# First layer opened by feature chunks, and layer 1's shift and scale as TensorE column products

## The chip, the cores and the metric

The kernel runs on one core of one Trainium2 chip. The metric is the device time of one execution in microseconds.

## The reference, cut to what matters

The whole program is two layers of `hybrid_layer` (the first block), followed by a second block of feed-forward and mixer stages that the change leaves alone. 256 rows, 1024 features, float32. Each of the two layers computes:

```python
def hybrid_layer(x, c, positions, norm_g, w_ada, b_ada, w_in, ...):
    mod = jax.nn.silu(c) @ w_ada + b_ada                  # (1, 1024) @ (1024, 3072)
    shift, scale, gate = jnp.split(mod[:, None, :], 3, axis=-1)
    h = rms_norm(x, norm_g) * (1 + scale) + shift
    z = h @ w_in                                          # (256, 1024) @ (1024, 2976)
    c_q, c_kv, k_rope, g_mla, q_b, k_b, v_b, g_moba = jnp.split(z, list(IN_OFFSETS), axis=-1)
    o_mla = mla_attention(c_q, c_kv, k_rope, ...)         # 8 heads, latents of 256 and 128
    o_moba = moba_attention(q_b, k_b, v_b, ...)           # 8 heads, one block of 256 keys
    y = concat([silu(g_mla) * o_mla, silu(g_moba) * o_moba]) @ w_out
    return x + gate * y
```

`mod` is one row of 3072 numbers for the whole layer; it needs all of w_ada (12 MB a layer). Its first third is the shift, the second the scale, the last the gate.

## The kernel before, in words

**Precision.** Every large product is made from three products of fp32r operands: x_high w_high + x_high w_low + x_low w_high. ScalarE writes the high part of a weights chunk (`wh`, L906, from `raw`), VectorE the low part (`wl`, L1529). A chunk is 128 partitions by up to 1024 numbers. Activations are split in the same way into `xt_h` (ScalarE) and `xt_l` (VectorE).

**Order of the work.** Each engine has its own program (`pe`, `act`, `dve`, `pool`, `sp`), written out in order; they meet in semaphores. `plan` lists all chunks in the order in which SP's queue loads them into the six `raw` buffers (`sp`, L2564): the load of chunk c waits until chunk c - 6 has been read. A list entry whose last field is set is a piece of w_ada. Such a piece isn't split: VectorE's `weigh` (L1552) multiplies it by a column of silu(c) and adds it to a row accumulator of 128 x 1024 numbers. There are five `wh`/`wl` buffers. `gemm` on TensorE takes the chunks one by one and, for each, the two row halves t = 0, 1 of the activations; results stand in banks 0/1 or 2/3 in turn, and ScalarE evacuates them. Banks 4 to 6 go round for small results (`rot`).

**`side` and `later`** are lists of small steps that all engines' programs hand out at the same points, a rate of steps behind each chunk. `side` carries attention, `later` carries w_ada's work for what comes next.

**The opening of layer 0.** SP loads 16 row pieces of w_ada (8 MB: shift and scale, j = 0 and 2, eight pieces of 1024 columns each), VectorE weighs them into `mkv`, TensorE turns the sums into columns (`turn_row`: four products of a 128 x 128 part with a column of ones each) and makes `keep_busy` products without use in between (5 and 3). x is loaded on ScalarE's queue as one DMA, normalised, transposed (`to_xt`), scaled and shifted per feature chunk into `xtmp`, and split into `xt_h`/`xt_l`. Then come four products one after another over all eight feature chunks: z (416 columns: the latents and k_rope), qb, kb, vb (512 columns each). The rotary tables (`reduce_angle`), head norms (`head_sums`, `head_scale`), the latents' transposes (`to_xt(("c", l) ...)`, `lower_latents`) and the bias table `mbias` are side steps beside these.

**Layer 1's w_ada.** `side_tiles` says what `later` weighs: during layer 0 the pieces (1, 0) into `qt`'s upper half, (0, 4), the gate of layer 0, into `acc`, and (1, 2) into `qkv`'s first rows, eight weighings each; four `turn_row` calls make columns of (1, 0) to (1, 3). During layer 1 the gate (1, 4). Layer 1's first instruction on the normalised rows (`affine`, `turned_row`) needs all its shift and scale.

**The rest of the layer.** Turn of the q and k heads (`turn_heads`), moba attention beside the four short mla products (q0, q1, kv0, kv1: 5 chunks' worth of small products, one take each), the gmla and gmoba gates (four chunks each), mla attention, the gate row and the two `out` products.

Of the kernel before, what the change touches and what calls it, by code (L numbers as in the profile page):

```python
# [15 lines left out]
DM = 1024  # L16
# [234 lines left out]
def build(nc, d, out, ctx):  # L251
# [122 lines left out]
    def stat(n, *name):  # L374

        if name not in stat_of:
# [10 lines left out]
    side_tiles = [[(1, 0), (0, 4), (1, 2)], [(1, 4)]]  # L387
    acc_of = {(0, 0): mkv[:, 0, :], (0, 2): mkv[:, 1, :], (0, 4): acc[:, :], (1, 4): acc[:, :],
              (1, 0): qt[:, 4:8, :].rearrange("p a b -> p (a b)"), (1, 2): qkv[:, 0, 0:DM]}
    acc_free = {(1, 2): ("tr", ("mobak", 0), 2), (1, 4): ("turn", 0, 5)}  # L390
# [9 lines left out]
    def weighed(l, j, kx):  # L400

        return ("acc", l, j + 1 if j < 4 and l == 0 and kx == 7 else j, kx)

    def first_bank_of(c):

        return {0: 2, 2: 3, 4: 7}.get(c)
# [60 lines left out]
    def pe(e):  # L467
# [76 lines left out]
        def to_xt(s, src, nch, ready, by="xl"):  # L544

            for c in range(0, nch, 2):
                m = min(2, nch - c)
                if s == ("x", 0) and first_bank_of(c):
                    b = open_bank(first_bank_of(c), (by, s, c + m - 1))
                else:  # L550
                    b = rot(by, s, c + m - 1)
# [92 lines left out]
        def rows_of_ada(l, j):  # L644

            wv = d["w_ada"][l].rearrange("(c p) n -> p c n", p=128)
            for kx in range(8):
                if len(plan) == c_no[0]:
                    plan.append((wv[:, kx:kx + 1, j * 512:j * 512 + 1024], 1, 1024, None, None, (l, j, kx)))
                c_no[0] += 1  # L650
                yield kx

        def ada(tiles):
            for i, (l, j) in enumerate(tiles):
                for kx in rows_of_ada(l, j):
                    yield
                    if kx < 2 and i:
                        turn_row(tiles[i - 1][0], tiles[i - 1][1] + kx)
                        yield
            for z in range(2):  # L660
                turn_row(tiles[-1][0], tiles[-1][1] + z)
                yield

        def turn_row(l, j):

            if j >= 4:
                return
            b = rot("mod", l, j)
            w.wait_ge(*at("acc", l, j // 2 * 2 if l else j, 7))
            w.wait_ge(*at("ones"))  # L670
            a = acc_of[l, j // 2 * 2][:, j % 2 * 512:j % 2 * 512 + 512]
            for f in range(4):
                last = mm(b[:, f:f + 1], a[:, f * 128:f * 128 + 128], ones[:, 0:1], True, True)
            last.then_inc(*up("turn", l, j))
# [3 lines left out]
        def keep_busy(n):  # L678

            w.wait_ge(*at("x"))  # L680
            for _ in range(n):
                mm(banks[0][:, 0:256], ident, h[:, 0, 0:256], True, True)


        b = rot("ccol")
        w.wait_ge(*at("id"))
        w.wait_ge(*at("c"))
        tr(b[:, 0:8], rows[0:8, :]).then_inc(*up("ctr"))
        list(rows_of_ada(0, 0))
        b = rot("cols")  # L690
        w.wait_ge(*at("rows"))
        tr(b[:, 0:n_rows], rows[0:n_rows, :]).then_inc(*up("rtr"))
        turn_row(0, 0)
        turn_row(0, 1)
        keep_busy(5)
        list(rows_of_ada(0, 2))

        ps, pts = Ring(pb1), Ring(pt1)
        for l in range(NL):
# [12 lines left out]
            else:  # L712
                to_xt(("x", l), lambda c, t: xn[:, t, c * 128:c * 128 + 128], 8, lambda c, t: [("xn", l, t)], by="xh")
                keep_busy(3)
                turn_row(0, 2)
                turn_row(0, 3)
# [4 lines left out]
            def ckey(t, kx):  # L721
                return ("c", l), kx

            later.add(ada(side_tiles[l]), 10 * len(side_tiles[l]))
            later.over(26 if l else 54)
            gemm(("z", l), XT, 0, xkey, win, 0, 416, "eva", head=STAG if l else 1,
                 soon=(lambda: turn_rows(1)) if l else None)
            if l == 0:
                b = rot("relb8")
                w.wait_ge(*at("rel"))  # L730
                w.wait_ge(*at("oh"))
                mm(b[0:8, :], relb[:, :], mq[0:32, 0, 0:512], True, True).then_inc(*up("relmm"))
            gemm(("qb", l), XT, 0, xkey, win, 928, 512, "eva")
            to_xt(("c", l), lambda c, t: z0[:, t, c * 128:c * 128 + 128], 3, lambda c, t: [("zn", l, t, 1)])
            gemm(("kb", l), XT, 0, xkey, win, 1440, 512, "eva")
            gemm(("vb", l), XT, 0, xkey, win, 1952, 512, "eva")
            side.drain()
            if l == 0:
                later.over(17)
# [3 lines left out]
                       lambda t: [("nrm", "kb", l, t)])  # L743
            side.add(attention("moba", l, lambda j: [("qk", ("mobaq", l), j), ("qk", ("mobak", l), j)],
# [19 lines left out]
            for j2 in range(2):  # L764
                o = open_bank(first_bank + j2, ("gate", l, j2))
                w.wait_ge(*at("acc", l, 4, 7))
# [1868 lines left out]
```

## Time and profile before

| | us |
|---|---|
| median of 3 runs | 1601.88 |
| lowest and highest | 1599.12, 2229.82 |
| the profiled execution, its own time | 1596.89 |
| the profiled execution, its span | 1594.7 |
| TensorE, VectorE, ScalarE busy | 1552.5, 1069.9, 869.8 |

The span runs from the first to the last instruction of the core; the execution's own time has 2.2 us more around it. Busy time of TensorE counts the records of its matmuls, which overlap: the distance between the starts of two records, not the length of one, is what a product costs in a stream. A product with float32 operands (not fp32r) leaves two records.

### The profile page before, as it was taken

To read this page: it belongs to the slowest core of one execution; us is meant where nothing else is said; L and a number is where in the kernel's file an instruction comes from. 1 tells how busy PE (TensorE), PEld (TensorE's weight loads), DVE (VectorE), ACT (ScalarE), POOL (GpSimd) and SP (SyncE) were. 2 spreads that over 40 slices of the span, in tenths; PEclk is the share of its full clock that TensorE was granted. 3 is DMA by queue.
4 is the path that set the end of the run, shared out by engine and by line. 5 is a ranking of instruction groups with operands and counts; after the bars stand their busy time and mean duration, and the time that the engine had idled before them with its cause. 6 is when DMAs were issued, how large, how long until landed. Compare 5 with 4: busy or idle time off the path is not lost.

```text
span 1594.7 us, 21371 instructions
## 1 busy us (share of the span) xinstructions
PE 1552.5 (97%) x7540; PEld 1290.8 (81%) x7540; DVE 1069.9 (67%) x1789; ACT 869.8 (55%) x1534; POOL 117.0 (7%) x142
## 2 busy tenths in 40 slices
PE   4989999999999999999999999999999999999998
PEld 4777887788888888888888888888888888888886
DVE  7987877666555766787756557565666578766553
ACT  3676667455445656565644446444566666554442
POOL 0310021011000000021000001000000002100000
PEclk9999999999999999999999999999999999999999
DMA  9964673379854634546565557975463444665651
GB/s 340 322 233 158 196 239 128 104 180 221 222 185 158 198 96 133 174 141 213 197 200 170 198 184 197 199 205 192 158 199 118 139 160 147 211 207 172 205 184 71
DMA packets 149026, 293.03 MB, mean 184 GB/s; under 512 B 10096, under 2 KB 23184, under 8 KB 148920
## 3 DMA queue, kind: packets, MB, share of 16 engines
q1 hardware_dynamic: 143424, 276.60, 51.5%
q0 software_dynamic: 4352, 12.15, 6.2%
q10 hardware_dynamic: 1144, 2.92, 0.5%
q8 instruction: 60, 0.98, 0.2%
q14 instruction: 46, 0.38, 0.1%
HBM read 290.57 MB, written 1.06 MB: 183 GB/s over the span
## 4 chain that ended last, share of the span: by engine, by line
PE 88%; DVE 5%; ACT 3%; issue 2%; DMA 1%; POOL 0%; DVEq 0%; SPq 0%; ACTq 0%
PE pb L475 83%; PE pb L479 5%; DMA raw<-in_w_ada 1%; DVE wl L1529 1%; ACT wh L906 1%; ACT pb L906 1%; DVE mkv L1526 1%; POOL st L2461 0%; DMA raw<-in_w_in 0%; DVE qt L1526 0%; ACT xt_h L906 0%; DVE mk L1529 0%; ACT mkv L906 0%; DVE B L1529 0%; DVE pb L1532 0%
## 5 line engine op out<-in xcount | busy, mean ns | idle before, releaser
L906 ACT ACTIVATE wh<-raw 128x1024 fp32r<-128x1024 f32 (+1 forms) x484 | 506.5, 1053 | 424.6 <-PE pb L475 394.2
L1529 DVE TENSOR_TENSOR wl<-raw,wh 128x1024 fp32r<-128x1024 f32 (+1 forms) x484 | 581.4, 1218 | 197.6 <-ACT wh L906 193.6
L475 PE MATMUL pb<-wh,xt_h 128*128 128x512 f32 (+2 forms) x1472 | 578.1, 393 | 4.0 <-ACT xt_h L906 2.5
L475 PE MATMUL pb<-wh,xt_l 128*128 128x512 f32 (+2 forms) x1472 | 572.4, 389 | 1.4 <-DVE xt_l L1529 1.0
L475 PE MATMUL pb<-wl,xt_h 128*128 128x512 f32 (+2 forms) x1472 | 569.6, 387 | 0.0
L475 PEld LDWEIGHTS pb<-wh,xt_l 128*128 128x128 f32 x1472 | 277.1, 188 | 64.1 <-DVE xt_l L1526 5.9
L475 PEld LDWEIGHTS pb<-wh,xt_h 128*128 128x128 f32 x1472 | 277.2, 188 | 59.5 <-issue 4.0
L475 PEld LDWEIGHTS pb<-wl,xt_h 128*128 128x128 f32 x1472 | 277.4, 188 | 52.5
L475 PE MATMUL pb<-wh,big_h 128*128 128x512 f32 x352 | 137.7, 391 | 0.0
L475 PE MATMUL pb<-wh,big_l 128*128 128x512 f32 x352 | 137.0, 389 | 0.0
L475 PE MATMUL pb<-wl,big_h 128*128 128x512 f32 x352 | 137.0, 389 | 0.0
L2461 POOL TENSOR_TENSOR st<-st,cols 128x1 f32<-128x1 f32 (+2 forms) x56 | 55.6, 1001 | 921.3 <-DVE st L1526 665.7
L475 PEld LDWEIGHTS pb<-wh,big_l 128*128 128x128 f32 x352 | 66.1, 188 | 13.8
L475 PEld LDWEIGHTS pb<-wl,big_h 128*128 128x128 f32 x352 | 66.1, 188 | 13.5
L475 PEld LDWEIGHTS pb<-wh,big_h 128*128 128x128 f32 x352 | 66.1, 188 | 13.4
L1526 DVE SCALAR_TENSOR_TENSOR sgt<-ti,pb 128x512 f32<-128x512 f32 (+1 forms) x48 | 30.3, 642 | 59.0 <-ACT ti L906 59.0
L1526 DVE SCALAR_TENSOR_TENSOR hid<-pb,few,sgt 128x512 f32<-128x512 f32 (+1 forms) x48 | 33.9, 706 | 46.8 <-PE pb L475 46.0
L906 ACT ACTIVATE p<-p,st 128x256 f32<-128x256 f32 x96 | 48.0, 501 | 28.4 <-DVE st L1532 28.4
L906 ACT ACTIVATE pt<-pb 128x512 f32<-128x512 f32 (+1 forms) x80 | 40.2, 502 | 28.8 <-PE pb L479 28.8
L906 ACT ACTIVATE big_h<-pb 128x512 fp32r<-128x512 f32 x44 | 24.1, 596 | 39.0 <-PE pb L479 39.0
L906 ACT ACTIVATE ti<-pb,few 128x512 f32<-128x512 f32 (+1 forms) x48 | 30.8, 658 | 18.4 <-PE pb L475 18.4
L2545 POOL TENSOR_TENSOR G<-G,mg 128x512 f32<-128x512 f32 x14 | 21.8, 1559 | 247.3 <-DVE mg L1526 247.0
(242 smaller groups left out, 1546.5 us busy)
## 6 DMA issues: line engine op xcount, KB each, us to landing
raw<-in_ffn_w_gu SPq DMA_DIRECT2D x160, 512.0 KB, 4.9
raw<-in_w_in SPq DMA_DIRECT2D x148, 512.0 KB, 4.3
raw<-in_ffn_w_down SPq DMA_DIRECT2D x88, 512.0 KB, 3.9
raw<-in_w_ada SPq DMA_DIRECT2D x48, 512.0 KB, 5.3
raw<-in_w_out SPq DMA_DIRECT2D x32, 512.0 KB, 4.1
raw<-in_w_branch SPq DMA_DIRECT2D x24, 512.0 KB, 4.2
raw<-in_ffn_w_gu SPq DMA_DIRECT2D x32, 256.0 KB, 4.9
raw<-in_w_in SPq DMA_DIRECT2D x8, 416.0 KB, 4.8
```

The costliest lines, as they stand in the source:

```text
L475: return e.matmul(o, a, b, start=start, stop=stop)
L479: return e.transpose(o, a, ident[0:n, 0:n])
L906: return e.activation(o, a, func, **kw)
L1526: return e.scalar_tensor_tensor(out=o, in0=a, scalar=s, in1=b, op0=op0, op1=op1)
L1529: return e.tensor_tensor(o, a, b, op)
L2461: e.tensor_tensor(stat(n, "rs", *name), v, halves.to_broadcast([128, n]) if n > 1 else halves, ALU.pow).then_inc(*up("rs", *name))
L2545: e.tensor_tensor(m, m, mg[mg_at(n, n0, t)][:, :], ALU.add).then_inc(*up("mrg", g, t))
```

## The change

The opening goes by feature chunks kx = 0 to 7. For each, SP loads two column blocks of w_ada (128 columns by all 1024 rows, one of the shift and one of the scale, in 512-byte pieces) and the chunk's rows of w_in for z (two chunks together, at even kx) and for q and k (1024 columns). TensorE makes the shift column straight from the raw block (eight products of a 128 x 128 block with a column of silu(c)); VectorE weighs the scale block into two partial sums of 128 x 128 that two products with ones add up. z, q and k are accumulated side by side in banks 0/1, 2/3 and 6/7 and finished together. vb follows, as before by itself. `keep_busy` is gone. x comes first on SP's queue, as two DMAs; ScalarE's rows DMAs are issued before its first Tanh.

Layer 1's shift and scale are 16 column blocks (`next_blocks`) that ScalarE's queue loads into `qkv[:, t, 0:1024]`, the tile of q and k once their heads are turned, two in turn; eight TensorE products make each column (`next_modulation`), as `later` steps from the q0 product on. The gate stays as rows on VectorE.

Around these, `reduce_angle`, gp and the rotary tables move ahead of the head norms, an activation table is loaded behind them, and the latents' transposes move behind the turn of the q and k heads. The core of the diff follows, first the shared tables, then TensorE's program (its `ada`, `next_modulation`, `opening` and the old opening that goes), then ScalarE's (`next_blocks`, `opening`), VectorE's `opening` and SP's first loads:

```diff
+    acc_free = [("modm", 7), ("turn", 0, 5)]
+    next_ada = [qkv[:, t, 0:DM].rearrange("p (c n) -> p c n", n=128) for t in range(2)]
+    N_LATER = (17, 8)
...
+        def ada(l):
+            for i in range(N_LATER[l]):
+                if i < 8:
+                    row_of_ada(l, i)
+                if i and l == 0:
+                    next_modulation(i - 1)
+                yield
+
+        def next_modulation(f):
+            b = rot("modn", f)
+            w.wait_ge(*at(f"next{f % 2}", f))
+            for cc in range(8):
+                last = mm(b[:, 0:1], next_ada[f % 2][:, cc, :], stat(8, "c_silu")[:, cc:cc + 1], cc == 0, cc == 7)
+            last.then_inc(*up("nextm", f))
...
+            for kx in range(8):
+                qk = weights(kx)
+                if kx < 7:
+                    blocks(kx + 1)
+                for t in range(2):
+                    xh, xl = (v[:, kx, t * 128:t * 128 + 128] for v in XT)
...
+                    w.wait_ge(*at("xh", ("x", 0), kx))
+                    for nm, i, c, o, hi, lo in parts:
...
+                        w.wait_ge(*at("hi", c))
+                        mm(o, xh, hi, kx == 0, False)
+                    for nm, i, c, o, hi, lo in parts:
+                        w.wait_ge(*at("lo", c))
+                        mm(o, xh, lo, False, False)
+                    w.wait_ge(*at("xl", ("x", 0), kx))
+                    for nm, i, c, o, hi, lo in parts:
+                        last = mm(o, xl, hi, False, kx == 7)
...
+                    if t == 0 and kx < 7:
+                        modulation_sums(kx + 1, modulation(kx + 1))
...
-        b = rot("cols")
-        turn_row(0, 0)
-        turn_row(0, 1)
-        keep_busy(5)
-        list(rows_of_ada(0, 2))
...
+        def next_blocks(f):
+            w.wait_ge(*at("nextm", f - 2) if f > 1 else at("tr", ("mobak", 0), 2))
+            wa = d["w_ada"][1].rearrange("(c p) n -> p c n", p=128)
+            e.dma_start(next_ada[f % 2], wa[:, :, 128 * f:128 * f + 128]).then_inc(*landed(f"next{f % 2}", f))
...
+            for kx in range(8):
+                w.wait_ge(*at("modk", kx, 1))
...
+                ac_(xt_h[:, kx, :], x_turned[:, kx, :], ACT.Identity, **affine).then_inc(*up("xh", ("x", 0), kx))
+                if kx >= 2:
+                    w.wait_ge(*at("xl", ("x", 0), kx - 2))
+                ac_(xtmp[kx % 2], x_turned[:, kx, :], ACT.Identity, **affine).then_inc(*up("xma", ("x", 0), kx))
+                split(stream.lead(3 if kx % 2 else 4))
...
+            for t in range(2):
+                q_(("qb", 0), t, banks[ACC_Q[t]])
+                squares(("qb", 0, t), qkv[:, t, 0:512], 512, [("eva", ("qb", 0), t)])
+                k_(("kb", 0), t, banks[ACC_K[t]])
+                squares(("kb", 0, t), qkv[:, t, 512:1024], 512, [("eva", ("kb", 0), t)])
+                z_(("z", 0), t, banks[ACC_Z[t]][:, 0:416])
+                split(stream.lead(1))
+            latent_squares(0)
...
+            for kx in range(8):
+                if kx:
+                    modulation(kx)
+                split(stream.lead(1 if kx % 2 else 2))
+                w.wait_ge(*at("xh", ("x", 0), kx))
+                w.wait_ge(*at("xma", ("x", 0), kx))
+                tt(xt_l[:, kx, :], xtmp[kx % 2], xt_h[:, kx, :].bitcast(F), ALU.subtract).then_inc(*up("xl", ("x", 0), kx))
+                if kx < 7:
+                    split(stream.lead(2))
+            split(stream.lead(2))
...
+            reduce_angle(0)
+            reduce_angle(1)
...
+        for t in range(2):
+            e.dma_start(h[:, t, :], d["x"][0, t * 128:t * 128 + 128, :]).then_inc(*landed(f"x{t}"))
```

## Rows read from the trace of the kernel before

**Rows 1.** The page's first part: busy us, share of the span, instructions of each engine

```profile
PE 1552.5 (97%) x7540; PEld 1290.8 (81%) x7540; DVE 1069.9 (67%) x1789; ACT 869.8 (55%) x1534; POOL 117.0 (7%) x142
```

**Rows 2.** Busy time by stretch: length, busy us per engine, TensorE clock, DMA share, GB/s

```profile
0.00:33.80 33.80, 14.28 (x66) 12.69 (x66) 23.08 (x34) 8.44 (x17) 3.98 (x12) 1.00 0.94 357
...
46.80:80.30 33.50, 33.50 (x152) 27.72 (x152) 32.05 (x65) 22.08 (x41) 13.13 (x12) 1.00 0.91 321
83.50:182.50 99.00, 93.08 (x515) 76.39 (x513) 80.94 (x180) 62.74 (x149) 7.92 (x6) 0.98 0.59 197
```

**Rows 3.** TensorE in order of time, 10 to 34 us: start, us, instruction, count

```profile
17.38 0.46 PE L479 MATMUL pb<-cst,rows 120*128 120x120 f32 x1 [11.85 <-DMA rows<-in_mla_k_g]
19.57 3.57 PE L475 MATMUL pb<-ones,mkv 128*128 128x1 f32 x16 [1.73 <-DVE mkv L1526]
...
27.41 2.76 PE L479 MATMUL pb<-cst,ob 128*128 128x128 f32 x16
...
31.31 1.84 PE L475 MATMUL pb<-ones,mkv 128*128 128x1 f32 x16
```

**Rows 4.** TensorE in order of time, 43 to 45 us, in the z product

```profile
43.73 0.46 PE L475 MATMUL pb<-wh,xt_l 128*128 128x416 f32 x1 [0.96 <-DVE xt_l L1529]
44.03 0.35 PE L475 MATMUL pb<-wh,xt_h 128*128 128x416 f32 x1
44.22 0.35 PE L475 MATMUL pb<-wl,xt_h 128*128 128x416 f32 x1
```

**Rows 5.** TensorE in order of time, 47 to 92 us: q product, heads, one turn_row

```profile
47.11 0.39 PE L475 MATMUL pb<-wl,xt_h 128*128 128x512 f32 x1
47.34 0.40 PE L475 MATMUL pb<-wh,xt_l 128*128 128x512 f32 x1
...
80.25 1.04 PE L479 MATMUL pb<-cst,qkv 128*128 128x128 f32 x8
...
90.80 0.95 PE L475 MATMUL pb<-ones,qt 128*128 128x1 f32 x8
91.61 0.48 PE L475 MATMUL pb<-wh,xc_h 128*128 128x512 f32 x1
```

**Rows 6.** Groups by form, 0 to 182.5 us: count, busy us, mean ns, idle before

```profile
L1529 DVE TENSOR_TENSOR wl<-raw,wh 128x1024 fp32r<-128x1024 f32 x29 | 35.1, 1219 | 0.8 <-ACT wh L906 0.8
L906 ACT ACTIVATE wh<-raw 128x1024 fp32r<-128x1024 f32 x29 | 30.4, 1057 | 14.4 <-DMA raw<-in_w_in 9.3 <-PE pb L475 5.2
...
L1526 DVE SCALAR_TENSOR_TENSOR mkv<-raw,st,mkv 128x1024 f32<-128x1024 f32 x12 | 15.4, 1284 | 4.4 <-DMA raw<-in_w_ada 3.6
...
L1526 DVE SCALAR_TENSOR_TENSOR mkv<-raw,st,mkv 128x512 f32<-128x512 f32 x4 | 2.8, 748 | 0.2
```

**Rows 7.** Loads, vectors and powers: queues and engines by time; page's DMA part last

```profile
0.74 22.12 SPq L2579 DMA_DIRECT2D raw<-in_w_ada  x16
...
11.16 0.33 ACTq L1104 DMA_DIRECT2D mq<-in_consts  x1
...
25.05 2.26 ACT L906 ACTIVATE ob<-h,st 128x1024 f32<-128x1024 f32 x2 [9.42 <-POOL st L2461]
...
24.45 1.68 POOL L2461 TENSOR_TENSOR st<-st,cols 128x1 f32<-128x1 f32 x2 [21.30 <-DVE st L1526]
...
raw<-in_w_ada SPq DMA_DIRECT2D x48, 512.0 KB, 5.3
```

**Rows 8.** ScalarE's groups by form, 33 to 182 us

```profile
L906 ACT ACTIVATE kt<-pb,gp 128x512 f32<-128x512 f32 x4 | 2.4, 690 | 1.4 <-issue 1.4
...
L906 ACT ACTIVATE xt_h<-z 128x256 fp32r<-128x256 f32 x4 | 1.4, 406 | 0.0
```

**Rows 9.** VectorE's angle chain from first to next instruction; ScalarE's table load

```profile
59.19 0.17 DVE L1523 TENSOR_SCALAR ang<-ang 128x32 f32<-128x32 f32 x1
...
60.85 1.22 DVE L1529 TENSOR_TENSOR wl<-raw,wh 128x1024 fp32r<-128x1024 f32 x1
...
87.80 1.28 ACT L906 ACT_TABLE_LOAD   x1
```

More of the change, by code:

```diff
@@ L398, in merged_by, with read_out @@
         return ("mrgv" if (n, n0, t) == (2, 512, 0) else "mrg", (s, "y", n, n0), t)
[L400 to L406, printed above, removed]
+    def read_out(what):
+        if what[0] == "shift":
+            return ("shm", what[1])
+        if what[0] == "scale":
+            return ("scs", what[1], 7)
+        return ("acc", *what)
     def moba_unit(l):
@@ L642, in attention, with row_of_ada @@
                 yield
-        def rows_of_ada(l, j):
+        def row_of_ada(l, kx):
             wv = d["w_ada"][l].rearrange("(c p) n -> p c n", p=128)
-            for kx in range(8):
[L648 to L674, printed above, removed]
-        pbuf = {}
[L678 to L682, printed above, removed]
@@ new lines, in pe, with modulation, modulation_sums @@
+        pbuf = {}
+        def modulation(kx):
+            c = shift_at[kx]
+            b = open_bank(4 + kx % 2, ("modk", kx, 1))
+            w.wait_ge(*at(f"raw{c % NRAW}", c))
+            w.wait_ge(*at("csil"))
+            for cc in range(8):
+                last = mm(b[:, 0:1], chunk_view(raw[c % NRAW], c)[:, cc, :], stat(8, "c_silu")[:, cc:cc + 1], cc == 0, cc == 7)
+            last.then_inc(*up("shm", kx))
+            return b
+        def modulation_sums(kx, b):
+            w.wait_ge(*at("ones"))
+            w.wait_ge(*at("scs", kx, 7))
+            for z in range(2):
+                last = mm(b[:, 1:2], part_sums[kx % 2][z], ones[:, 0:1], z == 0, z == 1)
+            last.then_inc(*up("modm", kx))
@@ L1104, in act @@
         e.dma_start(mq[0:32, 0, 0:512], d["consts"][0:32, C_OH:C_ROWS]).then_inc(*landed("oh"))
-        stream.lead(16)
-        rot()
-        turn_row(0, 0)
-        turn_row(0, 1)
+        w.wait_ge(*at("id"))
+        ac_(stat(1, "table"), ident[:, 0:1], ACT.Tanh)
+        w.wait_ge(*at("ccol"))
+        ac_(stat(8, "c_t"), cols[:, 0:8], ACT.Tanh, scale=0.5).then_inc(*up("ctanh"))
         def rows_squares(l, m, ready):
@@ L1216, in act @@
-            for t in range(2):
-                squares(("qb", l, t), qkv[:, t, 0:512], 512, [("eva", ("qb", l), t)])
-            gemm(("kb", l), XT, 8, 512, to(lambda t: qkv[:, t, 512:1024]))
-            for t in range(2):
-                squares(("kb", l, t), qkv[:, t, 512:1024], 512, [("eva", ("kb", l), t)])
-            if l == 0:
+                later.add(ada(l), N_LATER[l])
+                later.over(26)
+                gemm(("z", l), XT, 8, 416, to(lambda t: z0[:, t, :]), head=STAG, between=lambda: turned_row(1))
```

527 lines of the change are left out of this document (272 added, 255 removed).

## The prediction

> **What bounds the kernel now.** I read the page first: TensorE is busy for 97% of the span, VectorE for 67% [rows 1]. Such a share is an average, so the second view is busy time by stretch, cut where the code of the first block changes stage [rows 2]. Up to 33.8 us TensorE has nothing of its own to do: VectorE weighs rows of w_ada (23.1 us busy) and the DMA engines are at 0.94. From 33.8 to 46.8 it has small gaps, from 46.8 to 80.3 none (33.50 of 33.50), and from 83.5 to 182.5 it is idle for 99 - 93.1 = 5.9 us (80.3 to 83.5, the turn of the heads, stands between). So before 33.8 us TensorE time is free; behind it nearly every microsecond given to TensorE lengthens the span, and one taken from VectorE or ScalarE is worth at most part of those 5.9. Third, the order of TensorE's instructions gives the prices [rows 3 to 5]; fourth, ScalarE's and VectorE's groups by form give the chain that feeds it [rows 6, 8].
>
> The sums are made against the profiled execution (span 1594.7, its own time 1596.9, so 2.2 lie around the span). The median of the three runs is 1601.9, 5 us higher.
>
> **The start.** The change takes the h load off ScalarE's queue and puts it as two DMAs at the head of SP's. At one w_ada load every 22.12 / 16 = 1.4 us [rows 7] all raw loads land about 2.8 us later; hidden, because the weighting column c_silu is later still. ScalarE now issues its rows DMAs (5.78 to 11.49, 5.7 us) and the table load (1.28) before its first Tanh, so c_silu comes at about 9.6 instead of 6.4. In exchange the vectors land sooner: the last was issued at 11.2 and its transpose ran at 17.38 [rows 3, 7], 6.2 us on; issued at 7.2 it gives 13.4, with the transpose 14.0. VectorE's order puts cols and the variance behind that: 14.7. Two POOL powers are 1.68, one ScalarE scaling 1.15 (two took 2.26) [rows 7]: 16.7, with the second power beside it. Sixteen transposes at 0.17 (2.76 [rows 3]) end at 19.5. ScalarE's copy goes beside them; two products with ones (0.9 at the speed of the first sixteen) and VectorE's two column instructions (0.45) give shift and scale at 20.9. Then xt_h 0.42 and xtmp 0.33 on ScalarE (0.41 each alone [rows 8], less where they overlap), the z chunk's upper part 0.9, the q/k chunk's 1.0, its lower part on VectorE 1.15, xt_l 0.42, and the last three products of row half 0: 25.8. The modulation of chunk 1 follows. TensorE will then just have left an idle stretch: the sixteen one-column records at 19.57 took 3.57 us, the sixteen at 31.31 took 1.84 [rows 3], which are the levels 1.2 and 2.4 GHz (the view prints a granted clock of 1.00 there, but durations halve). I take something between: 2.4 for the modulation, 0.7 for its sums, modulation 1 ready at 29. The keep_busy products that are removed lay wholly in idle time, 3.5 to 6 us of it, and cost nothing now; without them the first steps run slow, up to 3 us, which is in the 29.
>
> **The eight steps.** One feature chunk is six z products at 0.19 (the spacing of 128x416 [rows 4]) and twelve q/k products at 0.2275 (0.23 in the pair shown [rows 5]): 3.87 us. The modulation adds eight 128x128 by one column products. In full stream eight records (four such products) took 0.81 us, from 90.80 to 91.61 [rows 5], so eight products are 1.65; two sums with ones and the two changes of kind make 0.55. TensorE alone would need 6.07 a step. The program's order is a chain, though. ScalarE makes xt_h, xtmp and only then the upper parts of this chunk's weights; VectorE's lower part follows; TensorE starts the next modulation only behind row half 0, and the next xt_h waits for it. Behind the sums: 0.45 (VectorE columns) + 0.42 + 0.33 + 1.0 + 1.15 + 0.42 + 0.65 (last three products) + 1.65 + 0.45 + some 0.3 of signals = 6.8 on odd chunks; even ones have 832 elements of z weights ahead, + 0.85 = 7.65. VectorE's weighing of a scale block is eight 128x128 instructions; the 512 and 1024 forms (748 and 1284 ns [rows 6]) extrapolate to 0.27 each, 2.15, which fits before the sums. DMA per step is 1.75 MB, 4.9 us at the 357 GB/s of the first 33.8 us [rows 2]. Six steps from 29: 3 x 6.8 + 3 x 7.65 = 43.4, so 72.4; the last chunk's row half 0 ends 4.6 later at 77, half 1 at 79. Before, the same three products (z, q, k) were finished at 69.3: the vb product, 48 x 0.2275 = 10.9, ends at 80.25 [rows 5].
>
> **Behind the steps.** vb uses banks 0 and 1, which hold z, and z is evacuated last on ScalarE, behind q, its squares, k, its squares, for each half. The squares of half 1 need a th tile that VectorE frees by its reduction, and VectorE stands behind two lower parts (2.3), both reduce_angle chains and gp (some 4.6 together: a chain ran from 59.19 to 60.85, 1.66 [rows 9], twice that, and 1.3 for the small instructions around, my estimate; before, they lay beside TensorE's products). That cover is gone: reduction at 84.0, squares, k, squares, z of half 1 at 86.3. vb half 1 starts there, and 9.55 us remain: 95.8 against 80.25, **+15.6**. The latents' transposes now stand behind the q and k heads, whose four kt copies are 2.4 us on ScalarE [rows 8]: first mla product about 5.0 us behind vb instead of 3.3, **+1.7**.
>
> **The layer.** Sixteen modulation columns of layer 1, each 1.65: 26.4 us of TensorE time in the stretch with 5.9 us idle. Removed are four turn_rows of 0.81 to 0.85: 3.4. **+23.0**. Off VectorE go 16 weighings of 0.75 to 1.28, half of them in this stretch; I credit 4 of the 5.9 idle us, with the Exp table load (1.28 at 87.80 [rows 9]) that moves to where vb waits anyway: **-4**. Each column waits for a 512 KB load that ScalarE issues one step earlier, behind the evacuation and the exponentials of that step; raw loads land in 5.3 us (median [rows 7]). In the four short mla products a step is about 4 us of TensorE, so two or three columns wait 2 to 4 us, with VectorE's mod instruction waiting behind and the softmax behind that; in the longer gate products they don't. **+6**, bounds 0 and 12.
>
> Sum: 15.6 + 1.7 + 23.0 - 4 + 6 = 42.3. 1596.9 + 42.3 = 1639 by the profiled execution; a median lies a little higher, so I say **1641**. Unshown operations: loads of 512-byte pieces (nearest: 1664-byte pieces at full rate and 256- to 512-byte vectors in the rows DMAs that took 6 us to land among others), from 0 to + 12 in all, value 0; 1024-piece issues on ScalarE, from 0.33 (the SP issue) to 1 us each, 16 of them beside TensorE work, from 0 to + 5, value 0.
>
> **A rule weighed.** The rows show that a one-column product costs 0.101 us per record in full stream [rows 5]. The Trainium skill (TensorE: Matmul & The Clock Gate, Back-to-back issue gap) gives about 60 cycles, 25 ns, between products of 1 to 64 columns. By it the layer's 256 records would be 6.4 us instead of 26 and the whole 1621, one of the rivals' ends; the trace disagrees, so I give it no more than part of the chance of rival 1.
>
> **Rivals.** (1) *TensorE-bound opening.* The chain overlaps better than I read it, half 1 fills it, and steps take 6.1; the evacuation stall is 2 instead of 6; columns fill the idle time of the layer without waits. Opening: 29 + 36.6 + 6.5 + 2 + 10.9 = 85, + 5; layer + 17: **1619**. For it: TensorE's own work is 6.07. Against: ScalarE's order is fixed. (2) *VectorE was the limit* (faster). In the layer VectorE is busy 80.9 of 99 us [rows 2]; if TensorE's densely packed products there really wait for wl at the pace of VectorE, taking 8 x 1.28 there and 8 x 1.28 in the opening away gives back up to 20, and the columns fall into the room: with an opening that ends level, **1588**. It decides if the weighings were on the path before; against it, the products of 46.8 to 80.3 are spaced evenly at 0.2275 and no row shows TensorE waiting for wl. (3) *Slow clock.* If TensorE stays at 1.2 GHz through the opening because every step has 1 to 1.5 us idle, a step is 12 instead of 7.2: + 34, **1675**. Against: the idle gap of 0.96 us before 43.73 left the 416-column products behind it at 0.35, spaced 0.19 [rows 4]. By the Trainium skill (same page, Part 1: The HAM clock gate) the gate goes by how busy the array has been; that is the way in which it could happen. (4) *Small pieces are slow.* At 200 GB/s a step's blocks take 5.2 + 1.8 = 7.0 and hide; at 120 GB/s 10.5: + 25 in the opening and + 10 in the layer, **1676**.
>
> **Chances.** Forecast 0.56, rival 1 0.27, rival 2 0.06, rivals 3 and 4 0.11. About 2% (32 us, 1634) is what a measurement of this kernel can tell from no change. The forecast's own range is 1625 to 1660, so some of it lies within 2%: faster 0.02, same 0.38, slower 0.60. The range 1613 to 1668 takes in most of rival 1 and leaves out rival 2 and most of 3 and 4.
>
> **What would show it.** First z product near 23 us and steps of about 7 us; VectorE's angle work between the last xt_l and the first reduction with TensorE idle some 5 us; vb over at 93 to 98; sixteen groups of sixteen one-column records of 1.6 to 1.9 us in the layer; layer 1's first z product at 220 to 230 instead of 183. I am wrong if vb ends before 88, if the columns' records are spaced much under 0.1 us, or if the layer grows by less than 15 us.

## The result and the profile after

The changed kernel takes **1661.37 us** (median of 4 executions, 1660.63 to 1661.95) against 1600.5 for the kernel before: a ratio of 1.0384, 95% interval 1.0363 to 1.0404. One of the four executions of the kernel before took 2229.82 us and is left out of the ratio. The prediction was 1641, with a range of 1613 to 1668: slower, as said, and 20 us too low. The time lies inside that range, but just outside the 1625 to 1660 that the prediction called the forecast's own. The profiled execution took 1660.86, its span is 1659.1 (64.4 more than before).

First the page of the changed kernel, its busy times and its TensorE clock in 40 slices of 41.5 us:

```profile
PE 1612.3 (97%) x7876; PEld 1346.5 (81%) x7876; DVE 1053.2 (63%) x1839; ACT 874.1 (53%) x1536; POOL 117.6 (7%) x142
...
PEclk8989989999999999999999999999999999999999
...
L477 PE MATMUL pb<-st,qkv 128*128 128x1 f32 x256 | 33.8, 262 | 8.8 <-DMA qkv<-in_w_ada 8.8
...
qkv<-in_w_ada ACTq DMA_DIRECT2D x16, 512.0 KB, 4.7
```

Beside [rows 1], TensorE has 60 us more and VectorE 17 less; the share of TensorE is 97% in both. The share doesn't show the loss; three marks in TensorE's order of time do. **A** is the first transpose of the heads (vb has ended), **B** the first mla product, **C** layer 1's first z product. In the kernel before, A stands at 80.25 [rows 5], B at 83.54 and C at 182.96, with 1411.7 us of span behind C. TensorE of the changed kernel in order of time, at the three marks:

```profile
104.31 1.99 PE L481 MATMUL pb<-cst,qkv 128*128 128x128 f32 x16
...
108.81 0.50 PE L477 MATMUL pb<-wh,xc_h 128*128 128x512 f32 x1 [0.38 <-ACT xc_h L963]
...
246.61 0.69 PE L477 MATMUL pb<-wh,xt_h 128*128 128x416 f32 x1 [0.90 <-issue]
```

| Stretch | Before | After | More | Predicted |
|---|---|---|---|---|
| start to A (opening) | 80.25 | 104.31 | 24.1 | 15.6 |
| A to B (heads, latents) | 3.29 | 4.50 | 1.2 | 1.7 |
| B to C (the rest of layer 0's first block) | 99.42 | 137.80 | 38.4 | 25.0 |
| behind C | 1411.7 | 1412.5 | 0.8 | 0 |

So nearly all that was lost stands where the prediction looked for it; the two large terms were too small by 8.5 and 13.4. Both stretches have much more half-speed time than those of [rows 2], in which the granted clock was 0.98 to 1.00. Busy time by stretch of the kernel before, cut at B and C, then of the changed kernel in its opening and at last between its own B and C (columns as in rows 2; the clock is the first number behind POOL's count):

```profile
83.54:182.96 99.42, 93.04 (x516) 76.39 (x514) 81.36 (x182) 63.16 (x150) 7.92 (x6) 0.98 0.58 196
```

```profile
22.40:31.00 8.60, 8.29 (x30) 7.16 (x30) 4.42 (x11) 1.33 (x2) 2.60 (x4) 0.50 0.53 170
31.00:39.00 8.00, 8.00 (x36) 7.00 (x35) 3.82 (x12) 2.04 (x3) 0.00 (x0) 0.68 1.02 266
...
54.50:62.50 8.00, 6.91 (x41) 5.46 (x40) 4.76 (x13) 2.83 (x4) 0.00 (x0) 1.00 0.93 269
...
92.20:104.30 12.10, 12.10 (x42) 9.70 (x43) 9.08 (x18) 8.78 (x21) 5.00 (x4) 0.78 0.46 133
...
108.81:246.61 137.80, 126.96 (x737) 109.89 (x737) 74.87 (x189) 62.70 (x148) 8.13 (x7) 0.89 0.53 164
```

In the layer the idle time of TensorE went from 99.42 - 93.04 = 6.4 to 137.80 - 126.96 = 10.8 us (+4.5), and its busy time went up by 33.9. A column here is the work for one column of layer 1's shift or scale: eight products, sixteen records. The columns and the price of a slow one are seen in TensorE's order of time, changed kernel:

```profile
119.51 3.54 PE L477 MATMUL pb<-st,qkv 128*128 128x1 f32 x16 [3.75 <-DMA qkv<-in_w_ada]
122.92 0.77 PE L477 MATMUL pb<-wh,xc_h 128*128 128x512 f32 x1
...
127.64 2.17 PE L477 MATMUL pb<-st,qkv 128*128 128x1 f32 x16
129.68 0.48 PE L477 MATMUL pb<-wh,xc_h 128*128 128x512 f32 x1
...
140.40 1.90 PE L477 MATMUL pb<-st,qkv 128*128 128x1 f32 x16
142.16 0.48 PE L477 MATMUL pb<-wh,xt_h 128*128 128x512 f32 x1
```

A column takes 142.16 - 140.40 = 1.76 us at 2.4 GHz and 3.41 at 1.2 GHz (119.51 to 122.92). The clock fell at 118.0, within the wait of 3.75 us that ends at 119.51, and rose at 128.2. Sixteen columns at 1.76 less the 3.4 of the turned rows are +24.8. What is left of the 33.9, 9.1 us, is a remainder; I put it down to work at half speed. The trace's clock fits that: it is at half for 29.7 us between B and C, against 3.6 in the kernel before. Half of the 26 us more would be 13, and in some of them TensorE is idle.

Waits for loads stand ahead of two of the five half-speed stretches of the layer: the 3.75 us above, and 4.57 us ahead of the last column (240.36), 19.4 us of half speed in all. The other three, 10.2 us, begin at 162.3, 199.9 and 217.0, each behind the sixteen records of a column, with no wait of TensorE above 0.5 us near them. The first of the three, in order of time and by stretch:

```profile
159.68 1.90 PE L477 MATMUL pb<-st,qkv 128*128 128x1 f32 x16
```

```profile
162.40:165.70 3.30, 3.30 (x17) 3.15 (x16) 1.74 (x3) 2.54 (x5) 0.00 (x0) 0.50 0.05 10
```

### The profile page after: what moved, and what is told of

It reads as the page before. It is cut to its first block, busy times and chain, and to the rows that moved or that the text cites. A ratio compares the mean times of both kernels' runs of the same rounds, so it can differ in the third digit from the quotient of the medians.

```text
span 1659.1 us, 22083 instructions
## 1 busy us (share of the span) xinstructions
PE 1612.3 (97%) x7876; PEld 1346.5 (81%) x7876; DVE 1053.2 (63%) x1839; ACT 874.1 (53%) x1536; POOL 117.6 (7%) x142
## 4 chain that ended last, share of the span: by engine, by line
PE 90%; ACT 3%; DVE 3%; issue 1%; DMA 1%; POOL 0%; ACTq 0%; DVEq 0%
PE pb L477 85%; PE pb L481 5%; ACT wh L963 1%; DMA qkv<-in_w_ada 1%; POOL st L2528 0%; DVE wl L1586 0%; ACT pb L963 0%; ACT th L963 0%; ACT L963 0%; DVE B L1586 0%; ACT dg L963 0%; DVE na_l L1583 0%; DVE acc L1583 0%; ACT kt L963 0%; ACTq L1147 0%
## 5 line engine op out<-in xcount | busy, mean ns | idle before, releaser
L477 PEld LDWEIGHTS pb<-wh,big_h 128*128 128x128 f32 x352 | 66.1, 188 | 13.4
L1583 DVE SCALAR_TENSOR_TENSOR hid<-pb,few,sgt 128x512 f32<-128x512 f32 (+1 forms) x48 | 33.9, 707 | 47.0 <-PE pb L477 46.1
L963 ACT ACTIVATE big_h<-pb 128x512 fp32r<-128x512 f32 x44 | 24.1, 596 | 39.1 <-PE pb L481 39.1
L477 PE MATMUL pb<-st,qkv 128*128 128x1 f32 x256 | 33.8, 262 | 8.8 <-DMA qkv<-in_w_ada 8.8
L477 PEld LDWEIGHTS pb<-st,qkv 128*128 128x128 f32 x256 | 33.6, 211 | 9.8 <-issue 8.7
```

The costliest lines, as they stand in the source:

```text
L477: return e.matmul(o, a, b, start=start, stop=stop)
L963: return e.activation(o, a, func, **kw)
L1583: return e.scalar_tensor_tensor(out=o, in0=a, scalar=s, in1=b, op0=op0, op1=op1)
```

## The experiments

All times are medians of 4 executions, beside the kernel before at 1598.1 to 1598.7 (7 executions each time). The marks are those of each kernel's profiled execution, which can be the fastest or the slowest of the four; where it matters, that is said. The diffs are against the changed kernel unless said.

**Part 2 alone.** The kernel before with only the layer's columns:

```diff
-                later.over(17)
+                later.add(cols_of_ada(), 17)
+                later.over(16)
```

with `next_modulation` and `next_blocks` as in the change, and the weighings of layer 1's shift and scale rows taken out.

> The kernel before with the second part of the change alone: its own opening, and layer 1's shift and scale as 16 column blocks loaded by ScalarE's queue and multiplied by TensorE from the q0 product on. If the two parts add up: the head transposes start at 80 us as before, the stretch from the first mla product to layer 1's first z product is 138 us as in the changed kernel (99 before), and the time is 1600 + 38 = 1638. If part of those 38 us came only from what the new opening leaves behind (late buffers, a low clock), the stretch is 125 or less and the time at most 1626.

Measured: 1633.33, ratio 1.022 (1.0205 to 1.0236), so +35. That is 5 us under the expected 1638; the stretch in the layer is the expected 138. TensorE in order of time, its first columns' wait, and the layer by stretch (B at 81.63, C at 219.07):

```profile
94.89 0.34 PE L477 MATMUL pb<-st,qkv 128*128 128x1 f32 x1 [5.85 <-DMA qkv<-in_w_ada]
```

```profile
81.63:219.07 137.44, 125.21 (x740) 107.91 (x738) 73.55 (x186) 64.28 (x150) 8.11 (x7) 0.91 0.55 169
```

The layer is 38.0 us longer, as in the whole change (38.4); A is at 79.25 and B at 81.63, 1.0 and 1.9 us earlier than before, so the span grows by 36.0. Part 2 alone thus costs 35 of the 61 us (by the ratios) and leaves 26 for the opening, which fits the 25.3 that the marks give it (24.1 + 1.2). The opening alone was not run, so that the two parts add up is worked out and not measured. The 5.85 us wait and the clock of 0.91 come without the new opening.

**A column of one product instead of eight** (seven eighths of layer 1's shift and scale sums are left out):

```diff
-            for cc in range(8):
+            for cc in range(1):
```

> The changed kernel with one product per column of layer 1 instead of eight (seven eighths of each sum are left out). Loads, waits and evacuations stay. Theory that the products and the low clock they bring are the cost of the layer: 7/8 of 26 us and 10 to 13 us of clock go, the layer falls from 138 to about 102 us and the time to 1625. Rival that the loads' waits hold the layer and the products lie inside them: less than 12 us go, time 1650 or more.

Measured: 1634.35, ratio 1.0223 (1.0206 to 1.024), 26 us less than the change by the ratios. By stretch between its B and C:

```profile
108.89:223.79 114.90, 98.22 (x512) 79.81 (x513) 73.85 (x189) 62.00 (x148) 8.13 (x7) 0.94 0.63 194
```

Busy time falls from 127.0 to 98.2 us: 28.7. The 112 products taken out (224 records) are 24.6 at 0.110; the rest, 4.1, fits less time at half speed. Idle time grows from 10.8 to 16.7, since the loads are now waited for in more steps (12.8 us in six waits). So the products' time was on the path, less some 6 us that come back as waits for the loads as soon as TensorE has less to do. The stretch falls by 22.9 in this profile, which is of the longest of that run's four executions (1639.31). The time came out between my theory (1625) and the rival (1650 or more).

**The operands exchanged** (c_silu's column as the weights, 128 columns of w_ada moving; the result then lies in one row and is not read as a column, so layer 1's shift and scale are other values):

```diff
-                last = mm(b[:, 0:1], next_ada[f % 2][:, cc, :], stat(8, "c_silu")[:, cc:cc + 1], cc == 0, cc == 7)
+                last = mm(b[0:1, 0:128], stat(8, "c_silu")[:, cc:cc + 1], next_ada[f % 2][:, cc, :], cc == 0, cc == 7)
```

> The changed kernel with the operands of layer 1's column products exchanged: the column of silu(c) is the stationary side and the 128x128 block streams through as 128 columns (the result is a row in one partition, so layer 1's shift and scale are not the reference's). The number of records and their spacing at full clock stay the same, about 0.11 us. Theory that the clock falls because one-column products leave the array nearly idle: the half-speed windows of the layer go, about 12 us less, time 1649. Rival that the clock falls because of gaps in which TensorE waits: no change, 1659 to 1663.

Measured: 1656.87, ratio 1.0364 (1.0349 to 1.038): 3 us less than the change by the ratios, with intervals that overlap, and between the 1649 of the theory and the 1659 of the rival. TensorE in order of time (B at 107.05, C at 240.42):

```profile
137.43 1.91 PE L477 MATMUL pb<-qkv,st 128*1 128x128 f32 x16
139.27 0.50 PE L477 MATMUL pb<-wh,xt_h 128*128 128x512 f32 x1
```

A column is 1.84 us instead of 1.76, so exchanging the operands gains nothing in the price. What it changes is the clock. Here are the changed kernel and this run, each from the end of its first half-speed stretch in the layer to the fall of the clock at the last column (by stretch):

```profile
128.30:237.30 109.00, 106.58 (x648) 92.10 (x647) 62.32 (x153) 50.99 (x116) 7.93 (x6) 0.95 0.52 161
```

```profile
123.40:235.90 112.50, 107.28 (x668) 83.54 (x667) 62.78 (x158) 52.66 (x122) 7.94 (x6) 1.00 0.55 165
```

The three half-speed stretches without a wait are gone: the clock is 1.00 throughout. The two at the waits for loads (3.59 us ahead of the first column, 4.42 ahead of the last) stay. So the theory and the rival each held for some of the stretches: in these two profiles the clock falls at the waits with either order, and behind a column only where it is made of one-column products. The other runs with one-column columns agree: part 2 alone has two such stretches without a wait above 0.3 us (from 136.7 and 174.2), and the run with one product per column has none. What these stretches cost in the median, 3 us, isn't clear of the noise.

A weight load of 128 columns is 107 ns by the Trainium skill (TensorE: Matmul & The Clock Gate, LDWEIGHTS), an estimate from its columns / 1.2 ns. The trace is near it in the first order at 2.4 GHz (0.110 us a record), but not at 1.2 GHz (0.213), nor in the second order (0.115), where one column is loaded.

**The column blocks issued one step earlier** (behind the turn of the heads for the first):

```diff
-                    if i < 16:
-                        next_blocks(i)
+                    if i < 15:
+                        next_blocks(i + 1)
...
+            if l == 0:
+                next_blocks(0)
             latents()
```

> The changed kernel with each column block's load issued one step earlier (the first right behind the turn of the k heads). Theory that the first column waits because its load is issued one step ahead only: the idle 3.8 us before the first column go, and if that idle time also causes the half-speed stretch behind it (118 to 128 us), another 4 to 5: time 1652. Rival that the clock falls by the products themselves: 1657.

Measured: 1650.19, ratio 1.0316 (1.0297 to 1.0335), 11 us less than the change by the ratios. The profile is of the fastest execution, 1644.41; the other three took 1650 to 1651, with a lower mean clock (0.984 against 0.987). The first columns and the layer by stretch (B at 106.75, C at 229.57):

```profile
114.36 1.99 PE L477 MATMUL pb<-st,qkv 128*128 128x1 f32 x16 [0.84 <-DVE st L1591]
120.27 1.90 PE L477 MATMUL pb<-st,qkv 128*128 128x1 f32 x16
```

```profile
106.75:229.57 122.82, 119.04 (x737) 102.06 (x737) 74.50 (x188) 62.68 (x148) 7.94 (x6) 0.97 0.59 183
```

The 8.8 us of waits for the blocks are gone, the busy time is 7.9 less with the same 737 instructions, and the clock is 0.97 instead of 0.89. The layer costs +23.4 here: 26.0 busy (24.8 for the columns, 1.2 at half speed) less 2.6 of idle time. The theory (1652) holds in kind: taking the waits away gave more than their own length. By how much more differs between the executions.

**Both: part 2 alone, one step earlier.**

> The kernel before with the layer's columns alone, whose blocks are issued one step earlier. Theory (without the waits and the half-speed stretches that stand behind them, 16 columns cost their TensorE time alone, 26 us less the 3.4 of the four turned rows): 20 to 25 us over the kernel before, no wait for the blocks over 1 us, time 1619 to 1624. Rival (the waits were not the cause of the lost clock, or the gain with the new opening came from elsewhere): over 1627.

Measured: 1624.43 (1622.14 to 1628.1), ratio 1.0161 (1.0142 to 1.018), 9 us below part 2 alone. The median is +25.7, just above the 20 to 25 of the theory and below the rival's 1627. The profiled execution is the longest of the four, and shows that the waits for loads aren't the one cause of the lost clock:

```profile
91.62 3.54 PE L477 MATMUL pb<-st,qkv 128*128 128x1 f32 x16 [1.74 <-DMA qkv<-in_w_ada]
99.75 3.52 PE L477 MATMUL pb<-st,qkv 128*128 128x1 f32 x16
```

```profile
82.47:214.36 131.89, 126.43 (x740) 108.03 (x737) 73.55 (x185) 64.57 (x150) 7.92 (x6) 0.91 0.57 177
```

The waits for blocks are 1.7 us in all, and still two columns and what lies between them ran at half speed: the clock fell at 90.4, in the wait of 1.74 us. TensorE had stood for 1.30 us just before that as well (87.7 to 89.0, for ScalarE's evacuation), a wait that the kernel before has too, without a fall of the clock. Of the 33.4 us more busy time 8.6 (33.4 - 24.8) are left for half speed. The same kernel was 6 us faster in another execution.

**The opening: splits ahead of the wait.** ScalarE and VectorE split this chunk's weights before they wait for its shift and scale (ScalarE's edit; VectorE's is alike):

```diff
             for kx in range(8):
+                if kx:
+                    split(stream.lead(3 if kx % 2 else 4))
                 w.wait_ge(*at("modk", kx, 1))
...
-                split(stream.lead(3 if kx % 2 else 4))
```

> In the opening, ScalarE and VectorE split this step's pieces of w_in before they wait for the step's shift and scale, not behind them. Theory (the steps of 7.2 and 8.0 us are a closed chain: shift and scale read, x weighed twice, w_in split by ScalarE, then by VectorE, the rest of x, then the next weighings, with TensorE's sum behind them; only about 2.1 us of ScalarE's split and 1.2 to 2.2 of VectorE's can leave it, and TensorE is busy 6.9 of 8.0 us behind it): steps of about 7.0, the first head transpose at 96 to 100 instead of 104.3, time 1652 to 1656. Rival (TensorE itself, or the pieces of w_ada and w_in arriving, sets the steps): the steps stay within 0.2 us, first head transpose at 103 or later, time 1659 to 1663.

Measured: 1655.73 (1650.94 to 1660.78), ratio 1.0357 (1.0327 to 1.0387); A at 99.98. The median moved as expected, but the interval does not separate it from the change. In the profile: the wait that the edit brought (ScalarE, then TensorE, in order of time), then the sums of the last chunks, whose distances are the steps:

```profile
38.08 1.06 ACT L963 ACTIVATE wh<-raw 128x1024 fp32r<-128x1024 f32 x1 [5.89 <-DMA raw<-in_w_in]
```

```profile
41.28 1.25 PE L477 MATMUL pb<-wh,xt_h 128*128 128x416 f32 x3 [3.14 <-ACT xt_h L963]
```

```profile
62.01 0.58 PE L477 MATMUL pb<-ones,acc 128*128 128x1 f32 x4
68.14 0.58 PE L477 MATMUL pb<-ones,acc 128*128 128x1 f32 x4
75.86 0.58 PE L477 MATMUL pb<-ones,acc 128*128 128x1 f32 x4
```

From sum to sum the six steps take 6.1, 11.1, 7.7, 7.7, 6.1 and 7.7 us, against 8.9, 8.0, 7.2, 8.0, 7.7 and 8.0 in the change. The two of 6.1 run at full clock and are TensorE's own work (6.07 in the prediction); each of the 7.7 has a half-speed stretch in it, and so has the 11.1. That one also holds the price of the edit: ScalarE now stands for a piece of w_in that landed late, 5.89 us, xt_h stands behind it in its order, and TensorE is idle for 3.14. So the six steps are only 1.3 us shorter in all (46.5 for 47.8); of the 4.3 us by which A is earlier, 0.7 lie ahead of them and the rest behind.

**The opening: z copied out first** (for both halves, ahead of q and k):

```diff
+            for t in range(2):
+                z_(("z", 0), t, banks[ACC_Z[t]][:, 0:416])
             for t in range(2):
...
-                z_(("z", 0), t, banks[ACC_Z[t]][:, 0:416])
```

> Behind the opening's products ScalarE copies both halves' z out first, before q and k. Theory (the 4.3 us for which TensorE stands at 92.15 is the wait for z half 1, which is fifth in ScalarE's order): that idle time goes, q and k come out about 1 us later, which is covered by products of z's successor; the first head transpose comes 3 to 5 us earlier (99 to 101), time 1656 to 1659. Rival (TensorE's next products wait for q and k's banks or for the next weights as well): less than 1.5 us is won, the idle time reappears under another releaser, time 1660 to 1662.

In the change the stall is this (TensorE; then ScalarE; then VectorE from the first angle instruction to its first reduction):

```profile
87.48 0.40 PE L477 MATMUL pb<-wh,xt_l 128*128 128x512 f32 x1
92.15 0.80 PE L477 MATMUL pb<-wh,xt_h 128*128 128x512 f32 x1 [4.27 <-ACT z L963]
```

```profile
89.85 0.63 ACT L963 ACTIVATE th<-qkv 128x512 f32<-128x512 f32 x1 [2.26 <-DVE st L1751]
...
91.60 0.50 ACT L963 ACTIVATE z<-pb 128x416 f32<-128x416 f32 x1
```

```profile
84.82 0.37 DVE L1580 TENSOR_SCALAR ang<-cst,st 128x16 f32<-128x16 f32 x2
...
89.15 0.67 DVE L1751 TENSOR_REDUCE st<-th 128x8 f32<-128x512 f32 x1
```

Measured with z first: 1659.85 (1652.7 to 1666.3; the profile is of the shortest), ratio 1.0383 (1.035 to 1.0416): nothing in the median. TensorE in order of time:

```profile
99.25 2.57 PE L481 MATMUL pb<-cst,qkv 128*128 128x128 f32 x11 [3.73 <-DVE qkv L1587]
```

The 4.27 us before vb's second half are gone, vb ends early, and TensorE waits 3.73 us for VectorE's normalised q instead (the transposes' first instruction, marked A, now stands behind a wait; B is at 106.94 against 108.81). The first transpose is at 99.25, as the theory said, but the idle time came back under another releaser and the median did not move, as the rival said. So with z out of the way it is VectorE's work on q (behind its angle work and reductions) that TensorE waits for.

**The opening: five products without use** ahead of the first z product, in idle time:

```diff
+        def keep_busy(n):
+            for _ in range(n):
+                mm(banks[0][:, 0:256], ident, h[:, 0, 0:256], True, True)
```

> Five plain 256-column products without use are added ahead of the first z product, where TensorE is idle. Theory (the half-speed stretch from about 22 to 36 us follows TensorE's idle opening, and costs 2 to 5 us of the first two steps because TensorE is busy in all of them): the product triplets are spaced 0.65 to 0.7 us from the start, the second sum comes 1 to 3 us earlier, the first head transpose at 101 to 103, time 1656 to 1660. Rival (the steps are set by the chain through VectorE and ScalarE, so TensorE's speed there is worth nothing, or the speed falls all the same): unchanged within 1 us, 1660 to 1662.

Measured: 1657.09 (1655.07 to 1660.01), ratio 1.0369 (1.0353 to 1.0384). The second chunk's shift and scale were read at 28.41 instead of 31.16, A came at 100.99. But in four other profiles in which nothing ahead of this point was edited they were read at 29.70, 29.74, 29.95 and 31.87, and in the run with all four edits, these products among them, at 30.46. So the edit may be worth 1 to 2 us there, and that is no more than one execution differs from another. Time, marks and sums came out as the theory said, but the runs can't tell the edit from chance: inconclusive.

**The opening: one product of eight in the shift columns of chunks 1 to 7** (seven eighths of their sums left out):

```diff
-            for cc in range(8):
+            for cc in range(8 if kx == 0 else 1):
```

> In the opening's steps 1 to 7 the shift column is made from one of its 8 products (7 x 7 products left out). Theory (a step is a closed chain in which, behind the rest of x, TensorE's three last products, the 16 records of the shift column at 1.84 us and the sums stand in a row of some 3.2 us, with VectorE's 2.1 us of weighings beside them): the chain shortens until the weighings end last, by about 1.0 us a step, so steps of 6.2 and 7.0 us, first head transpose at 96 to 98, time 1652 to 1655. Rival (the weighings or the arriving weights close the chain, the shift's products lie beside them): steps unchanged within 0.2 us, time 1659 to 1662.

Measured: 1652.05 (1647.27 to 1654.18), ratio 1.0322 (1.0298 to 1.0345); A at 97.39. Steps alternate between 6.6 and 7.4 us at full clock, where the change has 7.2 and 8.0. TensorE in order of time:

```profile
55.74 0.28 PE L477 MATMUL pb<-st,raw 128*128 128x1 f32 x2
56.84 0.61 PE L477 MATMUL pb<-ones,acc 128*128 128x1 f32 x4 [0.81 <-DVE acc L1583]
```

The shift products' time was on the path, but only 0.6 us a step of the 1.5 taken out: then VectorE's weighings of the scale block end last, with TensorE waiting 0.81 for them. Theory right, with 0.6 for its 1.0. A came 6.9 us earlier, more than six times 0.6: from the fourth of these sums (49.43) to the end of the products no half-speed stretch is left, where the change had one behind the sixteen records of a shift column (63.4 to 66.8), and the first of the sums came 2.4 us earlier.

**All four edits together** (blocks earlier, splits ahead, z first, the five products):

> The four edits together: column blocks issued one step earlier, w_in split ahead of the wait, z copied first, the added products. Theory (each has a place of its own): gains of about 11 (1650.2 was measured for the first), 7, 4 and 2 add up to 1636 to 1642, still slower than the kernel before by 2.3% or more, since the 16 columns' 26 us of TensorE work stay. Rival (a common limit, such as TensorE's own work in the opening, takes the place of the waits removed): 1644 to 1650.

Measured: **1642.92** (1641.56 to 1645.7), ratio 1.0281 (1.0265 to 1.0296), the best form with both parts, and still slower than the kernel before. By stretch, five of the steps (37.91 to 71.70) and then the layer (B at 102.06, C at 226.69):

```profile
37.91:71.70 33.79, 33.79 (x193) 30.54 (x192) 22.51 (x63) 13.39 (x18) 0.00 (x0) 0.90 1.02 303
...
102.06:226.69 124.63, 122.14 (x736) 104.68 (x737) 74.42 (x188) 62.78 (x148) 7.94 (x6) 0.94 0.58 179
```

TensorE is busy in 33.79 of 33.79 us. The steps take 7.7, 6.1, 6.1, 7.7 and 6.1 us: 6.1 at full clock, TensorE's own work, and 7.7 with a half-speed stretch. The layer costs +25. I expected 1636 to 1642, and 1642.92 lies between that and the rival's 1644 to 1650. Two of the gains that were added up did not show by themselves (z first, the five products), and TensorE's own work now bounds the steps, as the rival had it.

## Why the prediction came out 20 us low

**The start.** The first z product was predicted near 23 and came at 22.45. Chunk 1's modulation was to be ready at 29 and was at 30.9 (+1.9). I took 2.4 for its sixteen records, between the two levels, and 0.7 for its sums; both ran at 1.2 GHz:

```profile
9.84 3.54 PE L477 MATMUL pb<-st,raw 128*128 128x1 f32 x16 [4.37 <-DVE st L1580]
...
26.79 3.41 PE L477 MATMUL pb<-st,raw 128*128 128x1 f32 x16
30.05 0.99 PE L477 MATMUL pb<-ones,acc 128*128 128x1 f32 x4
```

They are 3.26 and 0.86 by the starts: 1.0 us more than I took. The 29 itself is not far off: in three of the four other profiles with nothing edited ahead of this point, shift and scale were read at 29.7 to 30.0 instead of 31.2. Whether the removed keep_busy products are the reason is not settled by the run with such products.

**The steps.** The chain that the prediction wrote out is the one that ran: VectorE's mod and ac, xt_h, xtmp, the weights' upper part, their lower part, xt_l, three products, the shift's products, the sums. Moving the splits out of it and taking products out of it both shortened the step, and with the splits moved TensorE bound it (6.1 us at full clock). In sizes, the predicted 6.8 and 7.65 were 7.2 and 8.0 (the column at 1.71 to 1.76 instead of 1.65, small gaps for the rest): 2.3 us over six steps. Two steps were longer, 8.5 and 7.7 for 7.2, by half-speed stretches: 1.7. Together 47.4 for 43.4.

**Behind the steps.** The angle work without cover was predicted to push z's second half to 86.3, that is 7.3 us behind the products' end; it ended at 92.10, 6.6 behind it, with TensorE idle for 4.27 and 0.74 (5 was said). Right in size, only later by the 5.9 above (92.15 for 86.3). From there vb's second half took 104.31 - 92.15 = 12.2, not 9.55: the clock in that stretch is 0.78. So 1.9 + 4.0 + 2.6 = 8.5, the whole difference of 24.1 to 15.6. The heads and latents: 1.2 for 1.7.

**The layer.** Column work +23.0 predicted, 24.8 measured: 1.76 instead of 1.65. Idle time: -4 and +6 predicted, together +2; +4.5 measured, of which the experiment without waits gives the two terms apart, -2.6 and +7.1. Both right in kind; but the prediction had all the waits in the short mla products, and the longest (4.57 us) stands ahead of the last column, near the end of the layer. The term that is not in the sum at all is TensorE's work at 1.2 GHz: 9.1 us, the remainder above. 1.8 + 2.5 + 9.1 = 13.4.

**What the working left out** is thus one thing: it priced each record at its full-speed duration behind the start, and gave the slow clock only as a rival in which it lasts through all the opening (1675). The other terms had the mechanism that ran. The slow clock came in pieces: about 1.0 + 1.7 + 2.6 us in the opening and 9.1 in the layer, 14 of the 22 us missing from the spans. The rest is the size of a column (1.8), the chain's small gaps (2.3), the start (0.9), the waits (2.5) and 0.8 behind C, less the 0.5 of the heads. [Rows 3] had both levels, the slow one where TensorE had been idle before. An added wait of 3 to 5 us in a dense stretch should have been priced at its own length and at what TensorE loses behind it. One run bears on that pair: with the blocks a step earlier, the 8.8 us of waits gave 11 by the ratios and 15.0 between the marks B and C. The stretches behind the columns, without a wait, no row shown ahead of the prediction has.

**The signs.** Of what the prediction said would show it, the first product, the idle time behind the steps and the columns' records came as said (two of the sixteen columns at half speed, one in part). Three did not: the steps took 7.2 to 8.5 us instead of about 7, vb was over at 104.3 instead of 93 to 98, and layer 1's first z product stood at 246.6 instead of 220 to 230. None of its three signs of being wrong appeared. Both large terms were too low, so that the time is in the range is owed to the range's width and not to errors that cancel.

**The rivals.** TensorE-bound opening (1619): not as the change stands, but its floor of 6.07 a step is reached at full clock (6.1) once the splits are moved. Slow clock (1675): not through the whole opening, but in pieces, as above. VectorE as the limit (1588): no; its busy time fell 6.5 us in the layer (81.36 to 74.87, the rows by stretch from B to C) and nothing came back but the 2.6 of idle time. Small pieces slow: no; layer 1's 512-byte pieces land in 4.7 us (median) where whole rows took 5.3 [rows 7], and their issue on ScalarE's queue takes 0.4 us. The issue gap of the Trainium skill (TensorE: Matmul & The Clock Gate, Back-to-back issue gap), by which the layer's records would be 6.4 us, doesn't hold for products that each load their own weights, and that section itself gives it as the gap of a product by itself. Here 256 records are 16 x 1.76 = 28 us, and taking 224 of them out gave 26 us.

**Open.** When a column lets the clock fall: of the sixteen in the changed kernel three did without a wait above 0.5 us, and the others did not. Why part 2 alone with early blocks lost its clock at 90.4, behind two short waits, of which the kernel before has the first. And single executions of one kernel differ by up to 14 us (z first: 1652.7 to 1666.3), where the kernel before keeps within 3.7; only one execution of each has a profile.

## What to carry to other kernels

Moving work from an engine with free time in its share (VectorE, 67%) to the one whose dense stretches make the span (TensorE) costs its full time, here 1.76 us for a 1024 by 128 column block in fp32, and 1.84 with the operands exchanged. With that exchange the clock stayed up behind the columns in the one profile taken, though the gain in the median (3 us) can't be told from noise. A wait that is added in a dense stretch of TensorE is to be priced with the half-speed time that can follow it (here 8.8 us of waits gave back 11 when taken away); issue the load one step earlier first. And when a stall is taken away, look for who is late next on the same engine: the z stall of 4.3 us came back as 3.7 us before the heads.

## What the runs showed of the hardware

The granted clock and the spacing of equal products agree: products 128x512 stand 0.43 us apart at 0.50 (123.91 to 124.34 in the changed kernel) and 0.23 at 1.00. Early in a trace they don't: the view prints 1.00 there though sixteen one-column records took 3.4 us (9.84 in the changed kernel, 19.57 before [rows 3]), since the trace's first clock record begins at 19.0 and 29.1 us. Before that, read the level from the spacing.

An fp32 product with one column on either side has two records of 0.110 to 0.115 us each at 2.4 GHz, whichever operand has the one column. Behind sixteen such records with one column moving the clock fell three times in the layer without a wait above 0.5 us; with 128 columns moving instead it did not in the one profile taken.
